# Second kind of layer: a new written order for the steps of projections, index, selection and four attentions on three engines

## The reference, cut to what matters

```python
def hybrid_layer(x, p_i, ...):                    # run twice (DEPTH = 2)
    proj = rmsnorm(x, g_pre_mix) @ w_in           # 1024 -> 3404 columns
    a_q, a_k, a_v, a_iq, a_ik, a_iw, b_q, b_k, b_v, b_f, c_q, c_k, c_v, d_q, d_k, d_v = split(proj)
    # a: index scores from rotated a_iq, a_ik and a_iw; the best 64 keys of each query; softmax over those
    # b: softmax with a decay from the running sum of log_sigmoid(b_f + b_forget)
    # c: two softmaxes per head, the second subtracted with a factor lam, then a norm of the rows
    # d: softmax in a window of 128 keys with a sink
    x = x + rmsnorm(concat(o_a, o_b, o_c, o_d) @ w_out, g_post_mix)
    h = rmsnorm(x, g_pre_mlp)
    x = x + rmsnorm(square(relu(h @ w_up)) @ w_down, g_post_mlp)
    return x + sigmoid(x @ w_ple_gate) * (p_i @ w_ple_proj)
```

## Time and profile before

| what | value |
|---|---|
| median of 3 runs | 1624.33 us (1623.91 to 1624.46) |
| profiled execution, its own time | 1623.88 us |
| its span in the trace | 1621.8 us |
| granted TensorE clock, mean | 0.973 of full |
| busy: PE, DVE, ACT | 1538.5 (95%), 1111.7 (69%), 811.2 (50%) us |
| share of the chain that ended last: PE, DVE | 77%, 8% |

### The profile page before, as it was taken

One profiled execution on the slowest core, in us unless ns is written; L12 is line 12 of the kernel. 1 busy time (PEld: TensorE's weight loads), 2 busy tenths in 40 slices (PEclk: granted clock), 3 DMA queues, 4 the chain that ended last, 5 costly groups with the idle time before them and its releaser, 6 DMA issues.

```text
span 1621.8 us, 26707 instructions
## 1 busy us (share of the span) xinstructions
PE 1538.5 (95%) x10572; PEld 1319.4 (81%) x10572; DVE 1111.7 (69%) x1623; ACT 811.2 (50%) x1303; POOL 20.8 (1%) x36
## 2 busy tenths in 40 slices
PE   7998979999999989899999899899999889899998
PEld 7997668888898856788889787788879778788886
DVE  3866677885476666688855887876454798777545
ACT  3533265664435334566544546655355346655334
POOL 0010100000001010000000000000000000000000
PEclk9999889999999989899999899999999999999999
DMA  7431035565553211556563332555545343456552
GB/s 254 152 118 60 24 104 169 167 214 197 168 169 101 80 30 61 183 167 215 188 190 114 113 103 96 175 189 195 198 165 164 104 105 104 130 184 201 199 182 104
DMA packets 185275, 236.62 MB, mean 146 GB/s; under 512 B 24480, under 2 KB 155328, under 8 KB 185024
## 3 DMA queue, kind: packets, MB, share of 16 engines
q1 hardware_dynamic: 182080, 230.18, 44.0%
q0 software_dynamic: 3072, 4.74, 1.1%
HBM read 232.78 MB, written 2.10 MB: 145 GB/s over the span
## 4 chain that ended last, share of the span: by engine, by line
PE 77%; DVE 8%; issue 6%; ACT 3%; DMA 2%; DVEq 2%; ACTq 1%; POOL 0%; SPq 0%; POOLq 0%
PE banks L440 76%; DVE all_ring_rounded L2814 2%; DMA all_ring<-in_w_in 1%; DMA all_ring<-in_w_ple_gate 1%; ACT all_ring_rounded L2632 1%; DVE all_rest L2983 1%; DVE all_work L2918 1%; DVE all_work L2880 1%; DVEq L2917 0%; POOL all_work L2093 0%; PE banks L2299 0%; DVE all_work L2902 0%; DVE all_work L2876 0%; PE banks L955 0%; ACT all_work L351 0%
## 5 line engine op out<-in xcount | busy, mean ns | idle before, releaser
L440 PE MATMUL banks<-all_work_rounded,all_ring_rounded 128*128 128x512 f32 (+2 forms) x4160 | 650.2, 318 | 13.3 <-DVEq L436 10.3
L440 PEld LDWEIGHTS banks<-all_work_rounded,all_ring_rounded 128*128 128x128 f32 (+1 forms) x4160 | 584.8, 190 | 76.6 <-DVEq L436 12.0
L440 PE MATMUL banks<-all_ring_rounded,all_work_rounded 128*128 128x512 f32 (+2 forms) x2304 | 501.8, 378 | 13.5 <-DVE all_ring_rounded L2814 10.4
L440 PEld LDWEIGHTS banks<-all_ring_rounded,all_work_rounded 128*128 128x128 f32 x2304 | 410.1, 192 | 95.9 <-DVE all_ring_rounded L2814 16.1
L2814 DVE TENSOR_TENSOR all_ring_rounded<-all_ring,all_ring_rounded 128x2048 fp32r<-128x2048 f32 x104 | 237.8, 2292 | 119.7 <-ACT all_ring_rounded L2632 117.4
L1641 DVE TENSOR_TENSOR all_ring_rounded<-all_ring,all_ring_rounded 128x2048 fp32r<-128x2048 f32 (+2 forms) x96 | 213.9, 2233 | 72.2 <-ACT all_ring_rounded L1388 70.5
L2632 ACT ACTIVATE all_ring_rounded<-all_ring 128x2048 fp32r<-128x2048 f32 x104 | 198.6, 1912 | 121.2 <-DMA all_ring<-in_w_mlp_down 86.8
L1388 ACT ACTIVATE all_ring_rounded<-all_ring 128x2048 fp32r<-128x2048 f32 (+2 forms) x96 | 177.8, 1859 | 103.3 <-DMA all_ring<-in_w_in 43.4
L440 PE MATMUL banks<-all_work 64*64 64x64 f32 (+8 forms) x2180 | 156.4, 272 | 23.5 <-ACT all_work L2636 9.1
L440 PEld LDWEIGHTS banks<-all_work 64*64 64x64 f32 (+5 forms) x2180 | 114.8, 153 | 58.6 <-issue 24.1
L440 PE MATMUL banks<-all_work,all_ring 128*128 128x128 f32 x704 | 102.1, 289 | 2.4 <-DVEq L409 1.9
(11 more groups left out here) (264 smaller groups left out, 1206.7 us busy)
## 6 DMA issues: line engine op xcount, KB each, us to landing
all_ring<-in_w_in SPq DMA_DIRECT2D x48, 1024.0 KB, 5.4
all_ring<-in_w_mlp_up SPq DMA_DIRECT2D x32, 1024.0 KB, 5.3
all_ring<-in_w_mlp_down SPq DMA_DIRECT2D x32, 1024.0 KB, 4.8
all_ring<-in_ffn_w_gate SPq DMA_DIRECT2D x22, 1024.0 KB, 5.4
all_ring<-in_ffn_w_up SPq DMA_DIRECT2D x22, 1024.0 KB, 5.6
all_ring<-in_ffn_w_down SPq DMA_DIRECT2D x22, 1024.0 KB, 4.9
all_ring<-in_w_out SPq DMA_DIRECT2D x16, 512.0 KB, 4.4
all_ring<-in_w_out SPq DMA_DIRECT2D x8, 1024.0 KB, 5.0
```

Of the source, the lines that this page charges most:

```text
L440: ins = self.nc.tensor.matmul(out, lhsT, rhs, start=start, stop=stop)
```

## The change

The three lists of `ORDER` in `block2` are written anew. Every step stays on its engine, with its instructions, and the order of steps within one part stays; what moves is how the parts are laced. On PE `panel`, `select` and `split` are empty steps, so their places say nothing. PE and DVE list by list:

```diff
     ORDER = {
         "PE": in_order("""
-            in:5 index select panel:2 select panel forget panel in:2 panel index panel c panel c in c in:2 forget:2 c:2
-            panel b in panel:2 c b c b panel b in c a:2 c b in split a b in panel in b a c a panel a in p a b in d panel
...
+            in:5 index forget:3 in:2 c:4 in b in index b:3 in:2 c:2 in c a b a:3 c:3 in b p in b:2 in a:2 d:3 a:2
+            early in:2 early:3 d rest d rest d late d:2 rest:2 late panel:15 select:2 split:3"""),
...
         "DVE": in_order("""
...
+            h panel:2 h in:5 panel forget:2 panel in index forget select in:4 panel c:2 panel b panel c:6 index
+            panel:2 b in b in:3 panel:2 b:5 a select a in a c:2 panel a:5 in:2 split:2 panel d:3 split panel:2 d:4 p d
...
```

More of the change, by code:

```diff
@@ L2270, in block2 @@
         "PE": in_order("""
-            in:5 index select panel:2 select panel forget panel in:2 panel index panel c panel c in c in:2 forget:2 c:2
-            panel b in panel:2 c b c b panel b in c a:2 c b in split a b in panel in b a c a panel a in p a b in d panel
-            d early:2 split early panel split rest d:2 early a d:2 rest late d rest:2 d late"""),
+            in:5 index forget:3 in:2 c:4 in b in index b:3 in:2 c:2 in c a b a:3 c:3 in b p in b:2 in a:2 d:3 a:2
+            early in:2 early:3 d rest d rest d late d:2 rest:2 late panel:15 select:2 split:3"""),
         "ACT": in_order("""
-            in panel in panel in panel select in:2 panel:2 index in:2 panel:2 index forget b in c select c:2 panel in
-            forget in panel in panel c:2 b panel c:2 in b panel forget in b c in a c b:2 split panel a in a:2 panel in
-            a:2 b a early split in c b a split p late rest early panel d:6 early rest d:2 late early rest:2"""),
+            panel:2 in:4 panel:2 forget:3 in index panel in:2 panel in panel c:2 in c:2 b:2 panel:2 index in:2 panel
+            b:2 in panel c:2 panel in c a:2 b c:3 in p b a:2 in b:2 in:2 a panel a d:2 a:2 panel:2 d:6 rest:4 select:2
+            early:4 split:3 late:2"""),
         "DVE": in_order("""
-            in panel in h panel h in:3 panel:2 forget in panel index select in index panel:2 in c:3 select in forget c
-            panel forget in b in c panel b c panel in c b panel in b c:2 a b:2 panel in a panel a in a:2 in split a
-            panel split early b c a d b split in d a d early d panel early rest late d:2 rest early d late d p rest:2"""),
+            h panel:2 h in:5 panel forget:2 panel in index forget select in:4 panel c:2 panel b panel c:6 index
+            panel:2 b in b in:3 panel:2 b:5 a select a in a c:2 panel a:5 in:2 split:2 panel d:3 split panel:2 d:4 p d
+            early:4 rest:4 late:2"""),
     }
```

## The result

| | before | changed |
|---|---|---|
| median of 4 runs (range), us | 1624.12 (1623.82 to 1624.46) | 1614.39 (1612.19 to 1617.30) |
| ratio, 95% interval | 1 | 0.9946, 0.9934 to 0.9958 |
| profiled execution, its span, us | 1623.88, 1621.8 | 1614.96, 1612.8 |
| mean granted clock | 0.973 | 0.978 |
| stretch of layer 20, of layer 21, us | 152.58, 152.71 | 148.09, 147.65 |

The change makes the kernel faster by 9.7 us between the medians (their quotient is 0.9940, inside the interval of the recorded ratio). The stretches give 4.49 and 5.06, 9.55 together; the spans differ by 9.0. From here on "stretch" is the time from the first matmul of the projection c_q to the first wide product.

What follows compares the result with a forecast made beforehand. PE, busy 95%, was taken as the bound, DVE nearly a second. Walking the three engines' lists gave 4.6 and 1.3 us per layer, taken as 6.1, 12.2 over two layers: 1612, range 1603 to 1622.

Steps and rivals of the forecast that it cites:

- Forget sums, b_q, b_k: Layer's first part: b_q and b_k move past the forget sums; PE's 4.60 us wait goes, 0.8 remains ahead of c's scores.
- The 4.60 has a cause that an order can remove: Fifth score tile of c: PE waited 4.60 us because ACT copied b_k out late, behind panel 7.
- Scores of c and c_v: PE does eight score tiles from 906.2 to 909.8, then projection c_v at full clock to 915.8.
- new wait on panel 6: After c_v and b's scores for t = 0, PE waits 2.7 us until DVE finishes panel 6 at 919.2.
- Clock: Behind the panel 6 gap: 1.7 us of PE work lost to slow clock, absorbed because panel 8 is done at 937.2.
- The rival built on 6.8, 1599.7: Old slow spell costs half its 13.6 us, so 12.3 us per layer are gained; chance 0.04.
- b_v and the cover of the selection: b_v at about 937.1; t = 1 selection, 9.9 us on DVE, covered by about 12 us of PE work, by 0.3.
- Only the releases move: Panel loads: SP's queue keeps its order; panel 9 has two microseconds of slack, panels 10 to 15 are looser; no cost.
- The tail: Behind the last output product: `p` ahead of d's last split, norm at 1004.6, unbroken 16.8 us DVE chain; 1.3 us gained.
- The second account: DVE's 12.36 us of waits per layer fall to 5.4, so 7.0 less; true value between that and 5.9.
- Given back: Rival: ACT's late answers cost DVE four waits of about 1.5 us, leaving no gain, 1624; chance 0.10.
- Panel 9's load: Slower rival: load landing over 9 us after release delays ACT and DVE, 7.6 us per layer lost, 1627.7; chance 0.08.

## Why the prediction was right, and where its sum was off

**The sign and the size.** 12.2 us were forecast and 9.7 measured, inside the range; the forecast time of 1612 is 2.4 below the measured median. By layer 5.9 to 6.1 were forecast, and 4.49 and 5.06 came; the stretches are 148.1 and 147.7, outside the 146 to 147 that was to be seen. Three terms below account for it, all to the same side: 1.2 for the late load in layer 20, 0.5 in the tail of each layer, and in layer 21 a slow spell longer by 1.0; other steps came a little sooner than walked. So one walk did not quite serve for both layers.

**Forget sums, b_q, b_k: as walked.** With the shift of 0.53 taken off, the scores of c start at 906.35 (forecast 906.2) after a wait of 0.95 (0.8), and PE's wait of 4.60 is gone.

**"The 4.60 has a cause that an order can remove": wrong as a price.** The copy of b_k was late, but moving it alone gave 0.1 and 0.3 us per layer. The cause that counted was on DVE: index t = 1 and two panels ahead of the maxima of c, as the rows of that kernel have it; no run moved these alone. The forecast total did not hang on it, because the walk let DVE's list set the times.

**Scores of c and c_v: right in sum, not inside.** I took the score products at the lengths of the earlier trace rows, 3.7 us; they took 1.71, because 20 of them had run at 0.50 before. PE then waited 0.92 for the first maximum, a wait that the walk lacked, and c_v started at 908.97 (unshifted) instead of 909.8. It ended sooner, so the **new wait on panel 6** was 3.46 instead of 2.7. The end of that wait, which is what counts, was forecast at 919.2 and measured at 919.08.

**Clock: 1.7 taken; 1.5 in layer 20, 2.5 in layer 21. "It is absorbed": right in layer 20, not in layer 21.** In layer 20 panel 8 was done at 936.9, and PE began b_v at 937.12: the spell was covered, as walked. In layer 21 panel 8 was done at 1317.6, PE began b_v only at 1318.53, and DVE's wait for PE ahead of the maxima of a grew from 1.20 to 1.85. When a_q took 7.43 there instead of 8.49, d_q's rotation came 1.06 us sooner. Two stretches of the changed kernel behind the gap, clock third from the end:

```profile
920.00:922.00 2.00, 2.00 (x11) 2.00 (x11) 1.71 (x4) 1.90 (x9) 0.00 (x0) 0.50 0.36 46
922.00:924.00 2.00, 2.00 (x14) 2.00 (x13) 1.93 (x3) 1.84 (x7) 0.00 (x0) 0.65 1.02 351
```

They lack 1.0 and 0.7 us of full clock, 1.7 together, and a_q took 1.5 more than c_v. Here PE was busy all through the spell. The rule of the Trainium skill (TensorE: Matmul & The Clock Gate, Terms), throttled time times one minus the ratio, gives 1.7 us for these rows, near the 1.5 measured. In the spell before, PE was partly idle, and the rule's 6.8 us is too much; but the 2.6 that the prediction set against it is too little. The spell also held the 20 score products, 2.92 us for what I estimate at 1.07 at full clock (20 of the 32 that took 1.71), so it cost about 4.5. The rival built on 6.8, 1599.7, did not come.

**b_v and the cover of the selection: right.** b_v at 936.6 unshifted (forecast 937.1), its wait gone, and d_q's rotation product at 966.5 with 0.20 us of waiting (966.6). "Cover enough" is what half a selection less confirmed: 0.6 us of 4.3.

**"Only the releases move ... panels 10 to 15 looser": this failed.** The slots for panel 15 are given back by a step of PE that does no product, and it had moved behind `early`. By the kernel that moves it back this cost 1.2 us in layer 20 and nothing in layer 21. In layer 20 it is the largest missed term. It kept the last output product from ending at 1009.1; it ended at 1010.02 unshifted. ACT also stood 2.03 us in front of panel 12 (950.75), which nobody waited for.

**The tail: 1.3 forecast, 0.8 measured** in layer 20 (13.61 less 12.81 us from the end of the last output product to the wide part). The chain was to be unbroken; it has one wait of 0.56 for ACT at 1019.84, and it took 17.35 instead of 16.8. ACT rounds two panels for 3.71 us from 1005.71 on, just as DVE's norm begins. The kernel with `p` last has the chain without that wait at 16.79. That the two panels are its cause I argue from these rows; no run moved them alone.

**The second account** said DVE's waits would go from 12.36 to 5.4; they are 7.76. What it missed are the 0.61 at 888.50, the 1.20 at 954.25, where DVE is ahead of PE, and the 0.56 for a panel's rounding. With the 1.20 the sign "DVE without a named wait from 890 to 1000" failed too. Its difference, 4.60, is close to the stretch's 4.49, though by the text the truth was to lie above the walk's 5.9.

**The rivals.** "Given back" happened in small: ACT's answers late, 1.38 on PE and 0.56 twice on DVE, in layer 20 1.2 of the 5.9 us forecast, instead of all of it. Panel 9's load did nothing: ACT waited 0.29 us for it at 925.37, and DVE not at all. Neither sign of being wrong came: PE's gap at 967 is 0.20, and DVE has no wait on L2643 or L2684.

## What to carry to other kernels

When several engines run written lists in order, ask of each wait whether the waiting engine is the one that is paid for: here closing a wait of 4.60 us on an engine that is busy 95% of the time gave nothing, because the other list was full up to the next meeting point, and of 3.46 us and the slow spell behind them no more could be had than the 1.20 and 1.85 us that the other engine in turn waited for this one further on. Look also whether the edit that closes a gap opens one on the other engine. A long step is cheap only where the engine that will need its result's bank or slot has as much other work ahead of that need, so move it together with the other engine's list and not alone (12.5 and 11.4 us lost per layer when alone). And count the steps that issue no work: one that only gives a buffer back held a load for 9.6 us here, at a price of 1.2 us in one layer and none in the other.

## What the runs showed of the hardware

- The same gap of 3.46 us ahead of a_q was followed by different slow spells. In layer 20 the granted clock was still 1.00 up to 920 and fell behind the gap, and a_q took 7.50 us. In layer 21 it was 0.50 from 1299 on, inside the gap, until 1305, and a_q took 8.49. At full clock it takes 6.02. In five more profiled executions with the same steps in this part, and the same gap within 0.01, it took 7.50 to 7.52 in layer 20, and in layer 21 8.41 to 8.65 and once 7.43.
- The price of a slow spell depends on what lies in it: d_v took 10.47 us behind a gap of 8.13 and 5.58 without one, nearly twice; c_v only 8.64 for 6.02 after a gap of 4.60, as the clock came back within it.
- A gap of 2.2 us ahead of the same output products was followed by a slow spell or not: with `p` last they took 4.61 us in layer 20 (gap 2.21) and 3.01 in layer 21 (gap 2.20).
- Two profiled executions of kernels that are the same outside the stretches differed by up to 5 us there (1314.5 and 1319.8). I found no cause. Edits worth 1 us per layer had to be read from the stretches, and there from the part that they touch.
